# State-space groups: cumulative sums by a DMA that repeats rows, and a clamp on ScalarE, in place of triangle and row-sum matmuls

## What is computed

```python
def step(state, inp):                       # one chunk of q = 128 tokens
    x_c, a_c, B_c, C_c = inp                # a_c = dt * A, never positive
    cum = jnp.cumsum(a_c, axis=1)
    cum_t = jnp.moveaxis(cum, 1, -1)
    seg = cum_t[..., :, None] - cum_t[..., None, :]
    decay = jnp.exp(jnp.where(causal, seg, -jnp.inf))
    cb = jnp.einsum('bign,bjgn->bgij', C_c, B_c)
    y_intra = jnp.einsum('bgij,bghij,bjghp->bighp', cb, decay, x_c)
    y_inter = jnp.einsum('bign,bghpn->bighp', C_c, state) * jnp.exp(cum)[..., None]
    ...
    return new_state, y_intra + y_inter
```

## Time and profile before

| what | value |
|---|---|
| median of 3 runs | 930.55 us (928.7 to 930.97) |
| span of the profiled execution | 928.9 us |
| PE busy | 918.9 us, 99% |
| PE weight loads busy | 849.6 us, 91% |
| DVE busy | 704.6 us, 76% |
| ACT busy | 564.9 us, 61% |
| POOL busy | 94.7 us, 10% |
| DMA | 175.53 MB, 189 GB/s on average |

### The profile page before, as it was taken

The page is one execution under the profiler, slowest core; times in us unless marked ns, Lnnn a source line. Parts: engine busy times, 40 slices in busy tenths (PEclk is TensorE's granted clock), DMA queues, the critical chain, the costliest instruction groups (busy, mean ns, idle before and its releaser), DMA issues.

```text
span 928.9 us, 17472 instructions
## 1 busy us (share of the span) xinstructions
PE 918.9 (99%) x6724; PEld 849.6 (91%) x6724; DVE 704.6 (76%) x952; ACT 564.9 (61%) x827; POOL 94.7 (10%) x82
## 2 busy tenths in 40 slices
PE   9999999999999999999999999999999999999997
PEld 6899999999899989989888888999879999999886
DVE  5957888889889968568777556679886798877663
ACT  4376655687877765456555345567675676666453
POOL 0000300024423300010000001303100100000001
PEclk9999999999999999999999999999999999999999
DMA  9954455577677756545655655535323365555661
GB/s 355 361 173 153 165 193 185 178 238 249 211 241 245 245 177 213 183 150 171 202 186 189 192 182 189 167 110 188 132 101 114 115 201 185 201 183 182 192 210 51
DMA packets 85565, 175.53 MB, mean 189 GB/s; under 512 B 5425, under 2 KB 46913, under 8 KB 85505
## 3 DMA queue, kind: packets, MB, share of 16 engines
q1 hardware_dynamic: 84384, 172.12, 54.8%
q10 hardware_dynamic: 752, 1.27, 0.5%
q0 software_dynamic: 368, 1.31, 0.4%
HBM read 173.63 MB, written 1.05 MB: 188 GB/s over the span
## 4 chain that ended last, share of the span: by engine, by line
PE 96%; DVE 2%; DMA 1%; issue 1%; ACT 0%; DVEq 0%; ACTq 0%; SPq 0%
PE proj_ps L1651 17%; PE proj_ps L1668 17%; PE proj_ps L1652 17%; PE proj_ps L1653 17%; PE proj_ps L1671 9%; PE proj_ps L1740 2%; PE aux L1781 2%; PE proj_ps L1741 2%; PE proj_ps L1742 2%; PE aux L1772 1%; DVE mod_acc L978 1%; PE aux L2074 1%; PE aux L2101 1%; PE aux L1756 1%; DMA raw<-in_panels 1%; PE aux L1796 1%
## 5 line engine op out<-in xcount | busy, mean ns | idle before, releaser
L966 DVE TENSOR_TENSOR w_lo<-raw,w_hi 128x1024 fp32r<-128x1024 f32 x276 | 341.5, 1250 | 125.9 <-ACT w_hi L477 125.4
L477 ACT CAST w_hi<-raw 128x1024 fp32r<-128x1024 f32 x276 | 286.1, 1047 | 175.2 <-PE proj_ps L1653 70.2
L1651 PE MATMUL proj_ps<-act_pair,w_hi 128*128 128x256 f32 x1016 | 289.9, 285 | 0.0
L1653 PE MATMUL proj_ps<-act_pair,w_lo 128*128 128x256 f32 x1016 | 287.3, 283 | 0.0
L1652 PE MATMUL proj_ps<-act_pair,w_hi 128*128 128x256 f32 x1016 | 287.3, 283 | 0.0
L1651 PEld LDWEIGHTS proj_ps<-act_pair,w_hi 128*128 128x128 f32 x1016 | 194.6, 192 | 3.6 <-issue 1.5
L1652 PEld LDWEIGHTS proj_ps<-act_pair,w_hi 128*128 128x128 f32 x1016 | 194.8, 192 | 0.6
L1653 PEld LDWEIGHTS proj_ps<-act_pair,w_lo 128*128 128x128 f32 x1016 | 194.7, 192 | 0.0
L1668 PE MATMUL proj_ps<-ff_pair,w_hi 128*128 128x512 f32 x256 | 69.9, 394 | 0.0
L1668 PE MATMUL proj_ps<-act_pair,w_hi 128*128 128x512 f32 x248 | 67.7, 394 | 0.0
L438 POOL TENSOR_TENSOR tmp_b<-tmp_b 128x512 f32<-128x512 f32 x4 | 5.2, 1293 | 461.2 <-ACT tmp_b L500 461.2
(11 more groups left out here) (353 smaller groups left out, 1640.6 us busy)
## 6 DMA issues: line engine op xcount, KB each, us to landing
raw<-in_panels SPq DMA_DIRECT2D x308, 512.0 KB, 3.9
mod_first<-in_panels SPq DMA_DIRECT2D x16, 512.0 KB, 10.0
xres<-in_x_t SPq DMA_DIRECT2D x2, 512.0 KB, 5.5
wst<-in_ws_t POOLq DMA_DIRECT2D x1, 512.0 KB, 3.7
bs_sb<-in_bs_rows POOLq DMA_DIRECT2D x1, 512.0 KB, 5.3
level_sb<-in_levels ACTq DMA_DIRECT2D x1, 512.0 KB, 5.3
out_t<-tmp_a SPq DMA_DIRECT2D x1, 512.0 KB, 2.6
out_t<-tmp_a SPq DMA_DIRECT2D x1, 384.0 KB, 3.0
```

What stands on the lines that cost most here:

```text
L477: nc.scalar.copy(w_hi[:, s, :], raw[:, s, :]).then_inc(hi_done, 1)
L966: tt(out=w_lo[:, s, :], in0=raw[:, s, :], in1=w_hi[:, s, :].bitcast(F32), op=ALU.subtract).then_inc(taken, 1)
L1651: mm(dst, hi, xh, start=first and k == 0 and nt % 2 == 0, stop=False, skip_group_check=True)
L1653: ins = mm(dst, lo, xh, start=False, stop=last and k == ks - 1, skip_group_check=True)
```

## The change

The cumulative sums of all heads and tokens are made once, before the convolution: one matmul gives them with tokens on partitions (`cum_col`), two give them with heads on partitions (`cum_t`), ACT copies both from PSUM, and a DMA writes `cum_t` to a buffer in DRAM. For every group, a DMA issued by ACT reads the group's 4 KB and repeats it on all 128 partitions (`cum_rows`, two buffers). ACT then makes `fall = max(0, cum_col - cum_rows)` with eight Relus (`decay_exponents`), which stands where the triangle did, since `cum` never rises; `decay` is exp of minus that, and `c_in` is exp of the rows themselves. The triangle products on POOL and ACT, and the six matmuls per group of L1912, L1913, L1916 and L1917, are gone. In ACT's order, `decay_exponents` for the next group stands after `split_hi` of slots 0 and 1, where `upto_low` stood before them. The diff, cut to its core:

```diff
-        a_upto_hi = at("a_upto_hi", 160, [2, HPG, P], F32R)
-        a_upto_lo = at("a_upto_lo", 183, [2, HPG, P], F32R)
-        after_r = at("after_r", 187, [P], F32R)
-        ones_r = at("ones_r", 187.5, [P], F32R)
+        cum_rows = [at("cum_rows_0", 160, [HPG, TT, P]), at("cum_rows_1", 183, [HPG, TT, P])]
+        fall = at("fall", 187, [TT, HPG, P])
...
-                for c in range(2):
-                    pool.wait_ge(S["seg_mm"], g * 2 + (c + 1))
-                    if c == 1:
-                        pool.wait_ge(S["cum_mm"], g + 1)
-                    settle(pool)
-                    for dst, part in ((a_upto_hi, a_hi), (a_upto_lo, a_lo))[:1 + first]:
-                        ins = nc.gpsimd.tensor_tensor(out=dst[:, c], in0=spread(part[:, c, bass.ds(g * HPG, HPG)].bitcast(F32), 2, P),
-                                                      in1=spread(upto, 1, HPG), op=ALU.mult)
-                    ins.then_inc(S["upto_ok"], 1)
...
-            act.wait_ge(S["dt_ok"], 1)
-            nc.scalar.copy(a_hi[:], dts[:, 1]).then_inc(S["a_hi_ok"], 1)
             act.wait_ge(S["wend_mm"], 1)
-            nc.scalar.activation(dts[:, 2, 0], aux[:, 1, 0:HEADS], ACT.Exp).then_inc(S["wend_ok"], 1)
+            nc.scalar.activation(dts[:, 2, 0], aux[:, 1, 0:HEADS], ACT.Exp)
+            nc.scalar.copy(cum_t[:], aux[0:HEADS, 1, T:2 * T])
+            nc.scalar.copy(flat(cum_col[:]), aux[:, 1, P:P + TT * HEADS]).then_inc(S["wend_ok"], 1)
             split_hi(xbc0, 2)
+            act.wait_ge(S["wend_ok"], 1)
+            act.dma_start(cum_d.rearrange("(h t) -> h t", h=HEADS), cum_t[:]).then_inc(S["cum_out"], 16)
...
+            def spread_cum(g, par):
+
+                act.dma_start(cum_rows[par][:].rearrange("p h c i -> p (h c i)"),
+                              cum_d[bass.ds(g * (HPG * T), HPG * T)].partition_broadcast(P)
+                              ).then_inc(S[f"cum_in_{par}"], 16)
...
+                    act.wait_ge(S["cum_out"], 16)
+                    spread_cum(0, 0)
...
-            def upto_low(g):
-
+            def decay_exponents(g, par):
+
+                act.wait_ge(S["ecum_ok"], g + 1)
+                act.wait_ge(S[f"cum_in_{par}"], (g + (2 - par)) * 8)
                 for c in range(2):
                     for h in range(HPG):
                         settle(act)
-                        nc.scalar.activation(a_upto_lo[:, c, h], upto, ACT.Copy, scale=a_lo[:, c, bass.ds(g * HPG + h, 1)].bitcast(F32))
+                        ins = nc.scalar.activation(fall[:, c, h], cum_rows[par][:, h, c], ACT.Relu, scale=-1.0,
+                                                   bias=cum_col[:, c, bass.ds(g * HPG + h, 1)])
+                ins.then_inc(S["fall_ok"], 1)
 
             def ssd_act(g, par, first=False, last=False):
+                if not last:
+                    act.wait_ge(S["ecum_ok"], g + 1)
+                    settle(act)
+                    spread_cum(g + 1, 1 - par)
                 act.wait_ge(S["cb_mm"], g + 1)
                 nc.scalar.copy(b_tok[:], aux[:, 1, T:T + P]).then_inc(S["btok_ok"], 1)
+                act.wait_ge(S["fall_ok"], g + 1)
                 for c in range(2):
-                    act.wait_ge(S["seg_mm"], g * 2 + (c + 3))
-                    nc.scalar.activation(flat(decay[:, c]), aux[:, 2 + c], ACT.Exp).then_inc(S["decay_ok"], 1)
+                    nc.scalar.activation(decay[:, c], fall[:, c], ACT.Exp, scale=-1.0).then_inc(S["decay_ok"], 1)
                 nxt = g + (GROUP["zg"] + 2)
                 landed_nxt = landed_group(nxt) if last else g * 2 + (zg0 + 3)
-                act.wait_ge(S["cum_mm"], g + 2)
-                nc.scalar.activation(flat(c_in[:]), aux[:, 0], ACT.Exp).then_inc(S["ecum_ok"], 1)
-                if not last:
-                    upto_low(g + 1)
+                nc.scalar.activation(c_in[:], cum_rows[par][:, :, 1], ACT.Exp).then_inc(S["ecum_ok"], 1)
                 split_hi(nxt, 0, landed_nxt)
                 split_hi(nxt, 1, landed_nxt)
+                if not last:
+                    decay_exponents(g + 1, 1 - par)
                 act.wait_ge(S["st_mm"], g + 1)
                 if not first:
...
+            decay_exponents(0, 0)
             ssd_act(0, 0, first=True)
...
-            mm(aux[:, 1, 0:HEADS], after, dts[:, 1, 0], start=True, stop=True).then_inc(S["wend_mm"], 1)
+            mm(aux[:, 1, 0:HEADS], after, dts[:, 1, 0], start=True, stop=True)
+            mm(aux[:, 1, P:P + TT * HEADS], upto, flat(dts[:, 1]), start=True, stop=True)
+            for c in range(TT):
+                ins = mm(aux[0:HEADS, 1, T + c * P:T + c * P + P], dts[:, 1, c], upto, start=True, stop=True)
+            ins.then_inc(S["wend_mm"], 1)
...
-                pe.wait_ge(S["ecum_ok"], g + 1)
+                if not first:
+                    pe.wait_ge(S["xdt_ok"], g)
...
-                for c in range(2):
-                    pe.wait_ge(S["upto_ok"], g * 2 + (c + 1))
-                    if c == 0:
-                        pe.wait_ge(S["y_ok"], g + 2)
-                    else:
-                        pe.wait_ge(S["mod_done"], mod + MOD_PAIRS_FIRST)
-                    mm(aux[:, 2 + c], after_r[:], flat(a_upto_hi[:, c]), start=True, stop=False)
-                    mm(aux[:, 2 + c], after_r[:], flat(a_upto_lo[:, c]), start=False, stop=True).then_inc(S["seg_mm"], 1)
                 zg_panel(1)
-                pe.wait_ge(S["xdt_ok"], g + 1)
-                mm(aux[:, 0], ones_r[:], flat(a_upto_hi[:, 1]), start=True, stop=False)
-                mm(aux[:, 0], ones_r[:], flat(a_upto_lo[:, 1]), start=False, stop=True).then_inc(S["cum_mm"], 1)
                 zg_panel(2)
...
+                pe.wait_ge(S["y_ok"], g + 2)
                 for h in range(HPG):
...
+                    pe.wait_ge(S["mod_done"], mod + MOD_PAIRS_FIRST)
                     pe.wait_ge(taken, g * (2 * SLOTS) + (zg0 + 3) * SLOTS)
                     mod_sum(ssd_cols, nts=range(4))
```

More of the change, by code:

```diff
@@ L145, in two_blocks @@
         stg = at("stg", 152, [2, 4, T])
[L146 to L149 removed]
+        cum_rows = [at("cum_rows_0", 160, [HPG, TT, P]), at("cum_rows_1", 183, [HPG, TT, P])]
+        fall = at("fall", 187, [TT, HPG, P])
         decay = at("decay", 164, [2, HPG, P])
         xdt = at("xdt", 168, [2, T])
+        cum_t = nc.alloc_sbuf_tensor_at("cum_t", [HEADS, T], F32, offset=16896 + 164 * 1024)
         c_in = at("c_in", 172, [HPG, P])
@@ L225, in two_blocks @@
         dts = at("dts", 194.5, [8, TT, HEADS])
-        a_hi = at("a_hi", 195.25, [TT, HEADS], F32R)
-        a_lo = at("a_lo", 195.5, [TT, HEADS], F32R)
+        cum_col = at("cum_col", 195.25, [TT, HEADS])
         mod_acc = at("mod_acc", 196.5, [1024])
@@ L234, in two_blocks @@
         upto, after, ident = (square[:, i, :] for i in range(3))
+        cum_d = nc.dram_tensor("cum_d", (HEADS * T,), F32).ap()
         proj_ps = ctx.enter_context(nc.psum_tensor("proj_ps", [P, 2, NT * T], F32))
@@ L254, in two_blocks @@
             "SGU": "v_ss v_rt v_ready sgu_mm sgu_y sgu_hi sgu_done",
-            "dt": "dt_mm dt_abs dt_exp dt_u dt_ln dt_ok a_hi_ok a_parts_ok sums_ok wend_mm wend_ok",
+            "dt": "dt_mm dt_abs dt_exp dt_u dt_ln dt_ok wend_mm wend_ok cum_out cum_in_0 cum_in_1",
             "convolution": "tap_act tap_dve conv_done xbc_done",
-            "SSD": "stg_ok upto_ok xw_ok cin_ok t_mm cb_mm seg_mm cum_mm st_mm y_mm xdt_ok cbm_ok m_ok y_ok "
+            "SSD": "stg_ok fall_ok xw_ok cin_ok t_mm cb_mm st_mm y_mm xdt_ok cbm_ok m_ok y_ok "
                    "btok_ok decay_ok ecum_ok state_ok",
@@ L618, in _ @@
                     conv_silu(c - 1)
-            act.wait_ge(S["sgu_done"], 1)
-            nc.scalar.copy(after_r[:], after)
-            nc.scalar.copy(ones_r[:], ones[:]).then_inc(S["sums_ok"], 1)
             def group_tiles(g, par):
@@ L700, in _ @@
             act.wait_ge(S["narrow_ok"], 1)
+            act.wait_ge(S["ecum_ok"], SSD_GROUPS + 1)
             for dst, src in ((rope_sb, rope_d), (level_sb, levels_d), (neg_sb, neg_d), (wgu, wgu_d), (wglr, wglr_d)):
@@ L1077, in _ @@
             nc.vector.memset(zero8[:], 0.0).then_inc(S["ready"], 1)
-            for n, (name, credit) in enumerate((("seg_mm", 2), ("cum_mm", 1), ("ecum_ok", 1),
+            for n, (name, credit) in enumerate((("ecum_ok", 1),
                                                 ("state_ok", 1), ("y_ok", 2), ("gs_mm", 1), ("gs_ok", 1))):
@@ L1149, in _ @@
             split_lo(GROUP["xbc"], 1)
-            dve.wait_ge(S["a_hi_ok"], 1)
-            tt(out=a_lo[:], in0=dts[:, 1], in1=a_hi[:].bitcast(F32), op=ALU.subtract).then_inc(S["a_parts_ok"], 1)
             split_lo(GROUP["xbc"], 2)
@@ L1956, in _ @@
                     pe.wait_ge(S["gdiag_ok"], q + 1)
-                    pe.wait_ge(*((S["ecum_ok"], 9), (S["gs_ok"], 9), (S["y_ok"], 10), (S["mod_done"], 6))[q])
+                    pe.wait_ge(*((S["xdt_ok"], 8), (S["gs_ok"], 9), (S["y_ok"], 10), (S["mod_done"], 6))[q])
```

3 lines of the change are left out of this document (removed).

## The result

The changed kernel takes 941.19 us (median of 4 runs, 940.75 to 944.82); the kernel before, beside it, 930.76 us (4 runs, 928.7 to 934.61). The ratio is 1.0121, with a 95% interval of 1.0097 to 1.0145: slower, by 10.4 us. The profiled execution spans 939.0 us, against 928.9.

The account below looks back on a forecast made before the run. It took an ACT, DVE and DMA loop through slot 1 to bound the groups, not PE: +7.6 us over six periods and +3.2 in the first group, 10.8 on 930.55, gave 941.3 us; range 932 to 952.

Parts of the forecast that it names:

- The main step: ACT in the groups: Relus moved behind the wait for slot 1's panel are exposed, 2.35 us per group.
- PE's saving: Six matmuls per group removed, 1.48 us each group, 11.8 us in all; PE stands idle, so it is not seen.
- The stage of the end weights: Before the convolution: three small matmuls and two exposed ACT copies that PE waits for, 1.05 us lost (bounds 0.6 and 1.6).
- The loop: From one gate Silu to the next through slot 1: mean period 19.0 us against 17.74, +7.6 us over six groups.
- S: The end of ACT's gate Silu (L646), a mark that returns once per group.
- L: From modulation panel 1's end, which frees slot 1, to ACT's cast of the next panel: 4.7 us, bounds 3.5 and 5.9.
- The second half: ACT from the start of slot 1's cast to the next S: 7.36 us plus 2.35 of Relus, 9.7 us.
- nothing: Near bound of the broadcast's delay to panel loads; far bound a further load's service, +10.5 us, a rival at 0.07.
- The 3.2 us per panel: Alternative panel landing, 2.0 us plus bytes over 436 GB/s; by it the loop takes 17.7 us, the change +2 us.
- Group 0: The first group's gate Silu ends at 209.9 against 206.77 us, +3.2 us, its Relus covering nothing.
- The zero for DVE: DVE's gain without POOL's products beside it, at most 3.5 us per group, falls after the second modulation panel: counted zero.
- PE leading: Rival: PE's 16.3 us of work per group sets the pace, -10.7 us, 919.9 us; chance 0.11, including a partial gain.

Follow-up runs that it names:

- after_no_broadcast_in_loop: The changed kernel in its own order, with the broadcast issued only for groups 0 and 1, later groups reusing those rows: 938.51 us.
- the last kernel: The changed arithmetic with all broadcasts during the convolution, Relus before the casts, gate Silu before slot 3's cast, each decay product one modulation panel earlier: 929.16 us.
- rows_ahead_in_zg: The changed kernel with all eight broadcasts issued during the convolution, seven into unwritten blocks of zg, and the Relus in front of the casts: 933.58 us.
- after_one_relu: The changed kernel with its order and broadcasts, but only one of the eight Relus made in groups 1 to 7: 933.99 us.

## Why the prediction was right

The forecast was 941.3 us; the median is 941.19. That the two agree within 0.1 us is luck: the four runs reach from 940.75 to 944.82 us, and several terms were off in opposite directions. The steps hold, but not all of them with the size they were given.

The main step held: ACT's order, not any engine's load, sets the time, and the Relus behind the slot casts are exposed. It was shown from both sides: moved behind the casts in the kernel before, the old products cost 7.8 us; moved ahead of them in the changed kernel, the Relus give back 5.6; seven of eight left out give 7.2.

PE's saving was worked out as 11.8 us and said to be unseen. PE's busy time fell by 5.5 us only, 918.9 to 913.4 (matmuls that run at half clock count for longer, which is likely the rest), and its waits in front of the y products came to 16 us. The two waits that were named, for `decay` and for `state`, are the two in PE's list, if the one that the trace leaves unnamed is `state`.

The stage of the end weights was estimated at +1.05 us. The changed kernel, from the first small matmul to the first of the SGU:

```profile
78.19 0.31 PE L1842 MATMUL aux<-dts,square 128*128 128x32 f32 x2
...
80.03 3.81 PE L1853 MATMUL aux<-wst,v_sb 128*128 128x128 f32 x32 [0.73 <-ACT cum_col L576]
```

That is 1.84 us, where the earlier trace rows have 79.55 - 78.87 = 0.68: +1.16 us. The estimate was near, and its wait of 0.73 us is below the 1.5 that would have spoken against it.

The loop, term by term. From S to the cast of slot 1 the forecast had 4.8 or 4.4 plus L = 4.7, a mean of 9.3; to the start of the second cast, slot 1's, the six periods show 9.81, 9.27, 9.90, 8.28, 9.62 and 8.37, a mean of 9.21 (the first is 219.79 - 209.98 in the timeline of group 1). The second half, 9.7, was 9.6. The period of 19.0 was 18.80.

Inside that 9.21 the working was wrong in two places that cancelled. L for slot 1 is 4.4 us in the mean (5.1, 4.5, 3.75, 4.7 and 3.85 in the five groups where it can be read), not 4.7. But the loads for slot 0 came late, which the forecast had not reckoned with: from the end of modulation panel 0 to their cast it is 5.1 to 6.7 us, and in group 3 slot 0 is the one that holds. The timeline of ACT there, and the landing times of line 296, from 190 to 340 us:

```profile
257.11 2.09 ACT L465 CAST w_hi<-raw 128x1024 fp32r<-128x1024 f32 x2 [3.50 <-DMA raw<-in_panels]
```

```profile
DMA to landing us min/median/max: 3.4/4.6/7.3
```

In the earlier trace rows they were 3.3, 4.4 and 5.7. The broadcast is issued just when these loads are, and "nothing" was the wrong value for it: the kernels without it put it at 2.7 us. That lies between the two ends that were given, nothing and 10.5 us. The 7.3 us is a load of group 0; from 209 to 325 us, without group 0, the panels land in 3.4, 4.5 and 6.4 us in the changed kernel and in 3.3, 4.0 and 5.0 us where the loop has no broadcasts (after_no_broadcast_in_loop). The Trainium skill (DMA: Bandwidth & Descriptors, "Issuing engines are not separate DMA queues") says that transfers started by ACT interleave with SP's on the same engines; the traces agree, with a longest panel landing of 6.4 us beside the broadcasts against 5.0 without them. The 3.2 us per panel that the prediction also worked out from the Trainium skill (same page, Anatomy of one DMA) goes by a fit that the page gives for transfers started by GpSimd; SP starts the panels, and the shortest landed in 3.4 us.

Group 0 was forecast at 209.9 and came at 209.98, and that was luck in part. (From 206.77 to 209.9 it is 3.1 us, not the 3.2 that the forecast's sum carries.) ACT there:

```profile
188.70 0.34 ACTq L598 DMA_DIRECT2D cum_rows<-cum_d  x1
188.82 1.05 ACT L465 CAST w_hi<-raw 128x1024 fp32r<-128x1024 f32 x1
...
192.12 0.24 ACT L672 COPY b_tok<-aux 128x128 f32<-128x128 f32 x1
...
199.25 2.25 ACT L465 CAST w_hi<-raw 128x1024 fp32r<-128x1024 f32 x2 [3.90 <-DMA raw<-in_panels]
```

`b_tok` came 1.1 us earlier than reckoned. The stretch began only 0.4 us later than before, not 1.05, and the DMA issue doesn't stand in its way: costed at 0.46 us in sequence, it goes out in 0.34 us while ACT is still at work on what is written before it, ahead of the cast and the Relus. The panels then landed later than the forecast's L: slot 0's cast starts at 199.25, after a wait of 3.90 us, and slot 1's at about 200.45 (199.25 + 2.25 - 1.05), some 6.1 us behind the end of modulation panel 1 where L was 4.7.

The zero for DVE is consistent with the runs. Without POOL's triangle products beside it DVE became faster, its modulation panels 1.41 us in the mean against 1.70, and the forecast's chain comes out without that gain; no run tested it alone.

Of the rivals, PE leading didn't come about. The price that it was given, -10.7 us, was too high even for its own case, and this is the part of the prediction that only the experiments could judge: it assumed that with the order mended PE would be next. Seven kernels with the changed arithmetic came out above the ranges expected of them, by 2 to 8 us. What was left out is the second loop, through slot 3, of 17.80 us, and behind it, at 17.4 to 17.5 us, some further chain. That this one, too, is made of landings in the ring (each slot is loaded twice in a group, and a load lands in 4.2 us at the median in the last kernel) is likely by ACT's waits for panels, 18.8 us there. It was argued from that row only and not shown.

## What to carry to other kernels

On an engine that works in order, what counts of an added operation is less its length than which wait it stands in front of or behind. Look for the last wait on a transfer in each period: work ahead of it is free up to the wait's length. Work behind it is paid, less what the later waits of the same loop take up: here 2.35 us per group, moved behind the wait, cost 7.8 us in seven groups, some 1.1 us in each. And where the leading engine has hardly a gap, check, before you count on a saving there, how long the loops through the other engines and the buffers take: here one of them, 17.80 us where it was read, was within 0.1 us of the period that PE had seemed to set, and a saving of 11 us was not to be had in any of the versions.

## What the runs showed of the hardware that was not expected

**TensorE's clock after a wait of about 2 us.** PE in the changed kernel, group 3, and windows of one projection panel in groups 3 and 4:

```profile
256.44 0.66 PE L1924 MATMUL aux<-decay,xdt 128*64 128x128 f32 x8 [2.17 <-DVE decay L1219]
257.03 0.42 PE L1652 MATMUL proj_ps<-act_pair,w_hi 128*128 128x256 f32 x1
257.25 0.41 PE L1653 MATMUL proj_ps<-act_pair,w_hi 128*128 128x256 f32 x1
```

```profile
257.03:261.96 4.93, 4.62 (x27) 4.45 (x25) 3.44 (x4) 4.85 (x13) 0.00 (x0) 0.65 0.73 235
276.11:279.25 3.14, 3.13 (x26) 2.93 (x24) 2.95 (x4) 3.14 (x9) 0.00 (x0) 1.00 0.69 236
```

After the wait of 2.17 us the matmuls start 0.21 us apart instead of 0.12: the granted clock is at its 1.2 GHz level for part of the panel, 0.65 in the mean, and the panel takes 4.93 us instead of 3.14. In group 1, after 1.93 us, it stayed at 1.00; in rows_ahead_in_zg it was 0.50 after 1.78 us. So a wait of 2.2 us cost PE some 1.8 us more in the panel behind it. In this group most of it was hidden: PE still waited 0.31 us at L1930 behind the slow panel, where in group 1, with the clock full, it waited 1.96.

**The beginning of an execution varies.** The same unchanged code, in the profiled executions of the change and of after_one_relu:

```profile
0.00:20.00 20.00, 17.87 (x77) 12.02 (x78) 10.09 (x23) 8.70 (x18) 0.20 (x4) 1.00 0.92 346
```

```profile
0.00:20.00 20.00, 17.72 (x57) 11.19 (x58) 9.97 (x22) 8.55 (x17) 0.20 (x4) 0.83 0.92 347
```

With a granted clock of 0.83 in the first 20 us instead of 1.00, PE did 57 matmuls there instead of 77 (in the next 20 us the clocks are 0.83 and 0.91), and the convolution's last activation came at 190.74 instead of 186.01 us. A difference of 4.7 us between two spans can be this alone, which is why the table above counts from a mark.

**One row on 128 partitions.** The broadcast of 4 KB to all partitions (512 KB written) lands in 4.2 us at the shortest and 6.8 at the longest, like a load of 512 KB, and takes ACT's queue 0.34 us to issue. In the groups, six of them cost 2.7 us; in the convolution, at a DMA share of 0.57, nothing.
